# Three rearranged loads in a one-core decoder block: a norm weight on GpSimd's queue, a quarter slot loaded after half of the attention rows, and an expert piece loaded in two halves

## Time and profile before

| | |
|---|---|
| median of 3 runs | 1225.13 us |
| the profiled execution | 1225.6 us, of which the span of the trace is 1223.2 us |
| TensorE busy | 1169.2 us (96%), matmuls |
| ScalarE, VectorE, GpSimd busy | 163.2, 309.4, 20.0 us |
| mean granted clock | 0.985 |
| data moved | 444.92 MB, mean 364 GB/s over the span |
| chain that ended last | 63% TensorE, 34% DMA |

### The profile page before, as it was taken

How to read it: one execution, slowest core, us unless ns; L and a number is a source line. 1 busy time by engine, 2 the same in 40 slices (tenths; PEclk the granted TensorE clock), 3 DMA queues, 4 the chain that set the end, 5 groups by cost and what they waited for, 6 DMA issues and landing times.

```text
span 1223.2 us, 16739 instructions
## 1 busy us (share of the span) xinstructions
PE 1169.2 (96%) x6720; PEld 553.2 (45%) x6721; DVE 309.4 (25%) x753; ACT 163.2 (13%) x278; POOL 20.0 (2%) x65
## 2 busy tenths in 40 slices
PE   9999999999999999999899999999999999999996
PEld 5854854876434334433333333343433333333342
DVE  4334553135411122211111111121211111111112
ACT  5312211144100001000000000000000000000001
POOL 3000010000000000000000000000000000000000
PEclk9999999999999999999999999999999999999998
DMA  8943400787999999999999999999999999999994
GB/s 282 383 144 116 138 10 1 271 290 302 416 422 410 435 431 430 425 428 428 430 427 431 431 433 430 430 432 431 430 432 434 430 429 430 431 431 424 425 427 191
DMA packets 44661, 444.92 MB, mean 364 GB/s; under 512 B 6452, under 2 KB 6916, under 8 KB 25800
## 3 DMA queue, kind: packets, MB, share of 16 engines
q1 hardware_dynamic: 43720, 441.63, 86.6%
q0 software_dynamic: 480, 1.85, 0.6%
q10 hardware_dynamic: 416, 0.79, 0.2%
HBM read 443.20 MB, written 1.05 MB: 363 GB/s over the span
## 4 chain that ended last, share of the span: by engine, by line
PE 63%; DMA 34%; SPq 1%; issue 1%; ACT 0%; DVE 0%; ACTq 0%; DVEq 0%
DMA ring<-in_w_gate_up 33%; PE bank L891 30%; PE bank L623 10%; PE bank L614 7%; PE bank L915 3%; PE bank L930 3%; PE bank L634 2%; PE bank L671 1%; PE bank L1038 1%; PE bank L906 1%; SPq L453 1%; PE bank L1029 1%; PE bank L862 1%; PE bank L826 1%; PE bank L807 1%; PE bank L840 1%
## 5 line engine op out<-in xcount | busy, mean ns | idle before, releaser
L891 PE MATMUL bank<-ring,region 128*64 128x512 f32 x3072 | 692.6, 605 | 40.8 <-DMA ring<-in_w_gate_up 39.9
L891 PEld LDWEIGHTS bank<-ring,region 128*64 128x64 f32 x3072 | 219.5, 139 | 469.4 <-issue 400.3
L1698 DVE TENSOR_SCALAR region<-bank 128x512 f32<-128x512 f32 x32 | 22.1, 692 | 578.5 <-PE bank L891 578.5
L623 PE MATMUL bank<-ring 128*128 128x512 f32 x288 | 125.9, 594 | 0.4 <-ACT ring L1089 0.4
L1089 ACT ACTIVATE region<-bank 128x512 f32<-128x512 f32 (+1 forms) x103 | 54.5, 529 | 387.0 <-PE bank L891 245.7
L614 PE MATMUL bank<-ring 128*128 128x256 f32 x384 | 84.1, 380 | 0.0
L623 PEld LDWEIGHTS bank<-ring 128*128 128x128 f32 x288 | 54.1, 190 | 64.8 <-issue 64.2
L1089 ACT ACTIVATE bank<-region 128x512 f32<-128x512 f32 x32 | 19.3, 602 | 457.8 <-DVE region L1698 457.8
L614 PEld LDWEIGHTS bank<-ring 128*128 128x128 f32 x384 | 72.7, 190 | 9.8
L915 PE MATMUL bank<-region 64*128 64x512 f32 x264 | 65.6, 615 | 0.3 <-ACT region L1089 0.3
L930 PEld LDWEIGHTS bank<-region,r_levels 128*128 128x128 bf16 x1584 | 63.1, 117 | 1.8 <-issue 1.6
(11 more groups left out here) (233 smaller groups left out, 547.3 us busy)
## 6 DMA issues: line engine op xcount, KB each, us to landing
ring<-in_w_gate_up SPq DMA_DIRECT2D x50, 4096.0 KB, 29.5
ring<-in_w_down SPq DMA_DIRECT2D x63, 2048.0 KB, 18.5
ring<-in_w_gate_up SPq DMA_DIRECT2D x24, 2048.0 KB, 17.0
ring<-in_w_in SPq DMA_DIRECT2D x6, 2048.0 KB, 17.7
ring<-in_w_xkv SPq DMA_DIRECT2D x4, 2048.0 KB, 10.6
ring<-in_w_gate_up SPq DMA_DIRECT2D x6, 1024.0 KB, 33.8
ring<-in_w_out SPq DMA_DIRECT2D x2, 2048.0 KB, 8.4
ring<-in_w_xq SPq DMA_DIRECT2D x2, 2048.0 KB, 8.5
```

The source lines that it names most:

```text
L623: last = pe.matmul(bk[:, :], lhs[:, k, t * P:(t + 1) * P], w[:, k, :], start=(k == 0), stop=(k == KT - 1))
L891: last = pe.matmul(bk[half * ROWS:(half + 1) * ROWS, :], lhs, w[:, half * 512:(half + 1) * 512], start=start, stop=stop, skip_group_check= ...
L1698: v.tensor_scalar(g_t, bank_g[:, :], LIMIT, None, ALU.min).then_inc(sem["g_clamped"], 1)
```

## The change

- `w_mix` is loaded from GpSimd's queue, right after `ident` has been built, instead of from SyncE's queue between the two halves of `x`. GpSimd's later constants come after it.
- `oT` is laid out (token half t, feature tile k, token i), so the first quarter of slot 9 holds token half 0 alone and is free once `xo00` and `xo10` have read it. `take_pv` writes that layout; the three loops that read `oT` use it.
- The first quarter of `(1, 3)` is loaded after `xo10`; only the two quarters D to 3D wait for `xw_ready`. `(1, 3)` thus comes in three loads.
- `(1, 5)` comes in two halves. The first waits for a new semaphore `lead_half`, raised by TensorE when the lead expert has finished the first feature tile of `(0, 0)`, for as many blocks as the table gives; the second waits for `chunk_used`, as the whole did.
- `nth_load` counts the loads of a piece by piece instead of by slot.

```diff
-IN_PARTS = {8: 2, 9: 2}
+IN_PARTS = {(1, 2): 2, (1, 3): 3, (1, 5): 2}
...
-        hT, yT, aT, oT = fm(region1), fm(region1), fm(region1), fm(region1)
+        hT, yT, aT = fm(region1), fm(region1), fm(region1)
+        oT = region1[:, :].rearrange("p (t k i) -> p t k i", t=NT, k=KT)
...
         def nth_load(e, k):
-            return loads_of[slot_of(e, k)].index((e, k)) + 1 + IN_PARTS.get(slot_of(e, k), 1) - 1
+            held = loads_of[slot_of(e, k)]
+            return sum(IN_PARTS.get(c, 1) for c in held[:held.index((e, k)) + 1])
...
             load_x(0)
-            sp.dma_start(w_mix, by_row(A["norm_mix_w"][0])).then_inc(sem["w_mix_in"], 16)
             load_x(1)
...
             load_chunk(1, 0)
+            wait_full(sp, "xo10")
+            load_cols(1, 3, 0, D)
             wait_full(sp, "xo01")
...
             sp.wait_ge(sem["xw_ready"], len(PIECES))
-            load_cols(1, 3, 0, 3 * D)
+            load_cols(1, 3, D, 3 * D)
...
             sp.wait_ge(sem["table_ready"], 1)
-            for e, k in order[RING:]:
+            blocks = sp.value_load(table[0:1, 0:1], min_val=1, max_val=MAXB)
+            sp.wait_ge(sem["lead_half"], blocks)
+            load_cols(*order[RING], 0, SLOT // 2)
+            used = sp.value_load(table[0:1, 2 * E + 1:2 * E + 2], min_val=0, max_val=CHUNKS * MAXW)
+            sp.wait_ge(sem["chunk_used"], sp.snap(used + 1))
+            load_cols(*order[RING], SLOT // 2, SLOT)
+            for e, k in order[RING + 1:]:
...
             pool.affine_select(out=ident[:, :], in_=ident[:, :], compare_op=ALU.not_equal, fill=1.0, base=0,
                                pattern=[[-1, P]], channel_multiplier=1).then_inc(sem["ident_ready"], 1)
+            pool.dma_start(w_mix, A["norm_mix_w"][0].rearrange("(p k) -> p k", k=KT)).then_inc(sem["w_mix_in"], 16)
...
-                by_token(f"xo{i}{t}", arrived("w_xo", i * PW), t, oT, needs)
+                w, bk = arrived("w_xo", i * PW), begin(f"xo{i}{t}")
+                for k in range(KT):
+                    await_rows(needs, k)
+                    last = pe.matmul(bk[:, :], oT[:, t, k, :], w[:, k, :], start=(k == 0), stop=(k == KT - 1))
+                end(last)
...
+                            if lead and (f, bk) == (0, 1):
+                                last.then_inc(sem["lead_half"], 1)
                         last.then_inc(sem["chunk_used"], 1)
...
             def take_pv(h):
-                take(f"pv{h}", oT[:, 2 * h:2 * h + 2, :], tiles(f"pv{h}", T))
+                take(f"pv{h}", oT[:, :, 2 * h:2 * h + 2, :].rearrange("p t a i -> p a t i"),
+                     bank_of(f"pv{h}")[:, :].rearrange("p (a t i) -> p a t i", a=2, t=NT))
```

More of the change, by code:

```diff
@@ L123 @@
  neg_max p_ready x2_squared x2_rms gu_part_ready gu_rest_ready router_scaled
- eT_part rank_psum h2T_part xw_ready cut_ready rest_ready panel_half scaled_ready rs_psum rs_ready gate_max gate_exps chosen_ready gates_ready up_gated
+ eT_part lead_half rank_psum h2T_part xw_ready cut_ready rest_ready panel_half scaled_ready rs_psum rs_ready gate_max gate_exps chosen_ready gates_ready up_gated
  nb_ready table_psum table_ready gT_psum gT_ready xb_rest
@@ L839, in _ @@
                     flip_rows("eT", 0, 1, "xo")
-                last = pe.matmul(bk[:, :], oT[:, k, P:T], w[:, k, :], start=(k == 0), stop=(k == KT - 1))
+                last = pe.matmul(bk[:, :], oT[:, 1, k, :], w[:, k, :], start=(k == 0), stop=(k == KT - 1))
             end(last, "xo01")
@@ L861, in _ @@
                         last.then_inc(sem["eT_part"], 1)
-                    last = pe.matmul(bk[:, 0:QUARTER], oT[:, k, P:T], w[:, k, c], start=(k == 0), stop=(k == KT - 1))
+                    last = pe.matmul(bk[:, 0:QUARTER], oT[:, 1, k, :], w[:, k, c], start=(k == 0), stop=(k == KT - 1))
                     if (q, k) == (1, KT // 2 - 1):
```

## The result

The changed kernel takes 1229.93 us (median of 7 runs, 1226.71 to 1231.64), the kernel before 1225.47 us in the runs beside it: ratio 1.0026, 95% interval 1.0014 to 1.0038, so 1.7 to 4.7 us slower. The forecast was 1224.6 us, 0.5 us less than the 1225.13 us from which it was worked out. A second measurement, in another set of runs, gave 1228.74 us against 1225.37, ratio 1.0029 (1.0017 to 1.0041). The profiled execution took 1231.6 us, with a span of 1229.6.

What follows compares the result with a forecast made beforehand. TensorE bounds until about 545 us, then the DMA at 430 GB/s, pinned to TensorE's clock at 391.11 us. 1225.6 - 0.5 (w_mix) - 0 - 0 = 1225.1 us profiled, 1224.6 for the median; range 1222.4 to 1226.6.

Steps and rivals of the forecast that it cites:

- Nothing from the two load changes: Early quarter of (1, 3) and halves of (1, 5): their advance is worth nothing at 391.11 us, so both count 0.
- the issue at 391 us: SyncE's 4 MB load at 391.11 us waits for slots TensorE frees, pinning the later DMA stream to TensorE's clock.
- The advance at 319 us: DMA ahead by 1.6 us at 319 us, 2.05 at most, from 0.8 us for each of the two load changes.
- the sign that the prediction had named: Rate in the three microseconds behind the issue at 391.11 us falls below 251 GB/s, as the DMA runs dry longer.
- The landing of w_mix: At the kernel's start, w_mix issued on GpSimd at 1.53 us lands at 4.6, 6.1 or 10.8 us; 5.4 taken.
- 0.5 us gained: Gain at the start from w_mix landing earlier on GpSimd's queue, kept to the end; at most 0.9 us.
- the 3.1 us row: Landing time of the smallest load on GpSimd's queue in the profile, used to estimate w_mix's landing.
- Rival B: w_mix lands late on GpSimd's queue, VectorE starting 0.3 or 5.0 us later: 1225.4 to 1230.1 us; chance 0.20.
- the 1.03 us: At the start, TensorE's first matmul stands 1.03 us behind VectorE's first instruction, at 6.76 us.
- the chance of "slower by over 0.2%" (0.06): Chance of a time above 1227.6 us, where the far end of the late w_mix landing lies.
- Case C: w_mix early, but first weight rows land 0.5 us later than 5.6, so TensorE starts as before: 1225.1 us; chance 0.20.
- oT by token half at no cost: ScalarE's copies of oT in runs of 128 elements count 0; at worst a few tenths of a microsecond.

Runs made afterwards that it cites:

- the pairs with equal starts: Kernel before and load changes alone, both with three extra matmuls: 1225.53, 1225.88 us; kernel before with w_mix on GpSimd and changed kernel, both with eight: 1227.57, 1227.56 us.
- the late quarter: Kernel before with (1, 3) loaded whole after xw_ready, its early quarter thus moved late: 1225.47 us, ratio 0.9997.
- the column alone: Kernel before with only the w_mix load moved to GpSimd's queue: 1229.23 us, ratio 1.0024.
- the column first on ScalarE: Kernel before with w_mix issued from ScalarE's queue, ahead of its load of the first weight rows: 1228.68 us, ratio 1.0022.
- The load changes alone: Changed kernel with w_mix back on SyncE's queue between the halves of x: 1227.38 us, ratio 1.0009.

## Why the prediction was wrong

- **Nothing from the two load changes: right**, to within about a microsecond. Shown by the pairs with equal starts (1225.53 and 1225.88, 1227.57 and 1227.56), by the late quarter that cost nothing, and by the profiles side by side: the issue at 391 us keeps its place behind TensorE's work, and by 398 us the DMA has moved as much as before. The path to it was not quite the one described. The advance at 319 us was about 0.4 us, not 1.6: the first half of (1, 5) went out a microsecond earlier (at 318.59 us, 314.5 with 4.08 us of shift taken off, for 315.64), but the DMA then waited for (1, 4), as the prediction said it might. And it was given back before 391 us, so the rate behind the issue did not fall clearly below 251 GB/s, the sign that the prediction had named.
- **The landing of w_mix: the step that failed first.** "So it lands at 4.6, 6.1 or 10.8 us ... I take 5.4". It landed at 7.64. The issue was 0.2 us later than worked out, and 5.9 us, not 3.9, passed to the landing. So the term "0.5 us gained" was a loss of 1.8 us at VectorE, and of about 2 us in the time when the pace is kept up. Nearness in size was the wrong guide: the 3.1 us row stands at 173 us, where the DMA was otherwise idle, and the start is full of loads. The row for a small load in that traffic was w_mix itself on SyncE's queue, 4.6 us; even that would have been too little.
- **The step that was missing: TensorE's pace.** The prediction let the wait of TensorE grow and priced it at its length. Rival B, which had the sign and the place, did so too and put a landing 1.8 us late at 1.8 us. The kernel before has the full clock from 4.98 us on, ahead of hf0; the changed kernel, idle for 2.13 us, got it only at 14.2, its four matmuls took twice as long, and 1.2 to 2.4 us came on top.
- **What made the column late on GpSimd's queue is not settled.** The Trainium skill, "DMA: Bandwidth & Descriptors", Latency and other measured facts, gives about 1 us to the first byte on GpSimd's path and 0.6 us on that of SyncE and ScalarE. The trace agrees with the sign and not with the size: 5.9 us from issue to landing for 4.6, 1.3 us more. On ScalarE's queue the column took 4.0 us ahead of 512 KB and 6.1 behind them, so place and traffic count as well; no run has it in the same place on two queues.
- **A misreading without consequence:** the 1.03 us that the prediction puts between VectorE's start and TensorE's first matmul is TensorE's idle time; the matmul starts 0.84 us behind VectorE (6.76 less 5.92), and 0.83 us in the changed kernel.
- **The range and the chance of "slower by over 0.2%" (0.06)** followed from the two failed steps. Case C did not occur: the weight rows landed at 5.9 us, in time.
- **oT by token half at no cost: right**, as far as the pairs show, since they hold it.

## What to carry to other kernels

A transfer that makes an engine wait in the first microseconds is to be priced by the landing times of loads in that same traffic, and each load ahead of which it is put must be priced as well: four places for 4 KB gave four ways to be 1 to 4 us slower. Where the stream of the DMA once ran dry for want of a free slot, earlier loads ahead of that point were worth nothing here, to within a microsecond; what shows it is the time of that issue and the bytes moved up to it, over several profiles, not one short window. And an idle time of TensorE is dearer than its length when the matmuls behind it come at the lower clock: look at the pace of the matmuls ahead of it too.

## What the runs showed of the hardware that I had not expected

TensorE began every profiled run at the lower clock: its first twelve matmuls, from 1.59 us on, take 2.93 us in all of them. When it rose differed, from 4.5 to 14.2 us. In the four profiles in which TensorE then stood idle for 1.98 to 2.91 us ahead of hf0 (the changed kernel twice, the column alone, the column first on ScalarE), the four matmuls took 3.35 to 3.75 us instead of 1.88 to 1.96: twice because the clock had not yet risen, twice because it had fallen again. But idle time is not all that decides. The load changes alone had 0.42 us of it and got the full clock at 10.87 us, and the late quarter, with the same instructions in the front, had 0.29 us and got it at 6.49:

```profile
6.86 1.95 PE L670 MATMUL bank<-ring 128*128 128x512 f32 x4 [0.29 <-DVE ring L1404]
```

What else decides was not tried. A profile's clock column can't be trusted ahead of its first entry; the durations of equal matmuls can.

With the 4 KB load put ahead of them on their queue, the 512 KB behind it landed about 2 us later than before, although the column's issue itself took only 0.4 us.
